# 512-column matmuls for block 1's queries and keys, last merge gates and four output projections, and for the DeltaNet and MoBA output projections

## The reference

```python
# block 1
xn = rmsnorm(h, norm_mix_g)
u = xn @ w_in
q, k, v, xr, gr, ga, gb = split(u)              # 1024 columns each
ya = chunked_band_attention(q, k, v, rel_table) @ w_attn_out
xc = causal_depthwise_conv(xr, conv_w, conv_b)  # 4 taps
hr = rg_lru(xc, w_rg_r, b_rg_r, w_rg_i, b_rg_i, rg_lambda)
yb = (hr * gelu(gr)) @ w_rnn_out
h = h + (sigmoid(ga + b_a) * ya + sigmoid(gb + b_b) * yb) @ w_o
h = h + (silu(g) * up) @ w_ffn_out              # g, up = split(rmsnorm(h) @ w_ffn_in)
# block 2, layer 0: gated DeltaNet; layer 1: MoBA attention
h = h + deltanet(rmsnorm(h)) @ dn_w_out
h = h + relu(rmsnorm(h) @ w_up[0])**2 @ w_down[0]
h = h + moba(rmsnorm(h)) @ mb_w_out
h = h + relu(rmsnorm(h) @ w_up[1])**2 @ w_down[1]
return rmsnorm(h)
```

## Time and profile before

| | |
|---|---|
| median of 3 runs (lowest to highest) | 1134.36 us (1133.88 to 1135.08) |
| the profiled execution | 1135.08 us, with a span of 1133.4 us |
| PE, DVE, ACT, POOL busy in the span | 99%, 67%, 52%, 19% |
| granted clock of PE | 0.999 |
| HBM | 164 GB/s mean |

### The profile page before, as it was taken

One profiled execution on the slowest core, in us unless ns is written; L12 is line 12 of the kernel. 1 busy time (PEld: TensorE's weight loads), 2 busy tenths in 40 slices (PEclk: granted clock), 3 DMA queues, 4 the chain that ended last, 5 costly groups with the idle time before them and its releaser, 6 DMA issues.

```text
span 1133.4 us, 21210 instructions
## 1 busy us (share of the span) xinstructions
PE 1121.4 (99%) x8546; PEld 1072.3 (95%) x8546; DVE 759.0 (67%) x931; ACT 590.0 (52%) x791; POOL 218.1 (19%) x216
## 2 busy tenths in 40 slices
PE   9999999999999999999999999999999999999997
PEld 9999989999888899999999988899999999889997
DVE  6656985676877744699885777754467657776442
ACT  6547557535555543665664556643355446665332
POOL 2995003302000000177843010000030002000000
PEclk9999999999999999999999999999999999999999
DMA  9774442655555555445410355555545445655541
GB/s 286 217 230 149 152 146 96 227 162 186 187 187 195 189 202 170 133 149 186 153 36 1 119 180 185 188 201 177 179 146 186 149 149 153 211 193 186 185 148 38
DMA packets 154995, 187.32 MB, mean 165 GB/s; under 512 B 6544, under 2 KB 143920, under 8 KB 154928
## 3 DMA queue, kind: packets, MB, share of 16 engines
q1 hardware_dynamic: 151360, 184.06, 49.8%
q10 hardware_dynamic: 3568, 2.31, 0.7%
HBM read 185.29 MB, written 1.07 MB: 164 GB/s over the span
## 4 chain that ended last, share of the span: by engine, by line
PE 87%; POOL 5%; DVE 5%; issue 1%; ACT 1%; DMA 0%; DVEq 0%; POOLq 0%; ACTq 0%
PE PS L445 18%; PE PS L386 16%; PE PS L387 16%; PE PS L388 16%; PE PS L447 9%; POOL XN L891 2%; DVE WL L382 2%; POOL TAP L889 2%; POOL XN L886 1%; PE PS L452 1%; PE PS L453 1%; PE PS L454 1%; PE PS L1988 1%; PE PS L2001 1%; PE PS L755 1%
## 5 line engine op out<-in xcount | busy, mean ns | idle before, releaser
L382 DVE TENSOR_TENSOR WL<-RAW,WH 128x2048 fp32r<-128x2048 f32 x170 | 399.9, 2354 | 225.3 <-ACT WH L373 225.2
L373 ACT ACTIVATE WH<-RAW 128x2048 fp32r<-128x2048 f32 x170 | 324.9, 1911 | 227.3 <-PE PS L388 208.1
L445 PE MATMUL PS<-XHL,WH 128*128 128x512 f32 x864 | 300.9, 395 | 0.0
L386 PE MATMUL PS<-XHL,WH 128*128 128x256 f32 x832 | 240.6, 289 | 2.6 <-DVE WL L333 1.4
L447 PE MATMUL PS<-XHL,WL 128*128 128x256 f32 x864 | 239.8, 278 | 0.0
L387 PE MATMUL PS<-XHL,WH 128*128 128x256 f32 x832 | 236.2, 284 | 0.0
L388 PE MATMUL PS<-XHL,WL 128*128 128x256 f32 x832 | 236.2, 284 | 0.0
L445 PEld LDWEIGHTS PS<-XHL,WH 128*128 128x128 f32 x864 | 162.1, 188 | 37.6
L388 PE MATMUL PS<-HH,WL 128*128 (+1 forms) x688 | 194.9, 283 | 0.0
L386 PE MATMUL PS<-HH,WH 128*128 (+1 forms) x688 | 194.9, 283 | 0.0
L387 PE MATMUL PS<-HL,WH 128*128 (+1 forms) x688 | 194.9, 283 | 0.0
(11 more groups left out here) (305 smaller groups left out, 1634.9 us busy)
## 6 DMA issues: line engine op xcount, KB each, us to landing
RAW<-in_mlp_w_up SPq DMA_DIRECT2D x32, 1024.0 KB, 5.4
RAW<-in_mlp_w_down SPq DMA_DIRECT2D x32, 1024.0 KB, 5.0
RAW<-in_w_in SPq DMA_DIRECT2D x25, 1024.0 KB, 5.1
RAW<-in_w_ffn_in_pairs SPq DMA_DIRECT2D x22, 1024.0 KB, 5.1
RAW<-in_dn_w_in SPq DMA_DIRECT2D x16, 1024.0 KB, 5.7
RAW<-in_mb_w_in SPq DMA_DIRECT2D x12, 1024.0 KB, 5.1
RAW<-in_w_ffn_out SPq DMA_DIRECT2D x11, 1024.0 KB, 5.0
RAW<-in_w_attn_out SPq DMA_DIRECT2D x4, 1024.0 KB, 5.8
```

The lines of the kernel that those rows point to most:

```text
L373: act.activation(WH[:, k], RAW[:, k], ACT.Copy).then_inc(hi_done, 1)
L382: dve.tensor_tensor(WL[:, k], RAW[:, k], WH[:, k].bitcast(F32), ALU.subtract).then_inc(lo_done, 1)
L386: pe.matmul(out, wh, xh, start=start, stop=False, skip_group_check=True)
L445: pe.matmul(out.rearrange("p (e t) -> p e t", e=2), h[:, k, part], XHL[:, :, k], start=(k == 0), stop=False, skip_group_check=True)
```

## The change

`multiply_wide` gets the two halves of its moving operand as an argument (`both`), the hook `beside` of `multiply`, and a form with the old products (`halves_` false), used for ro 3. It is called for qk 0 to 7, gab 4 to 7, ao, ro, wo, do and mo, with banks in pairs by the table PAIRS. OH and OL, and DOH and DOL, become halves of one tensor each. The recurrent gates' results go to banks 0 and 1, no longer 3 and 4. ACT copies the right half (`low_to`) to LT, a new buffer of three places in the room of VT (qk), to GAB (gab), or to MU (ao, ro 0 to 2); DVE adds the left half there (`add_to`), and the old read-out works on this sum, out of SBUF. ro 3 is read from its banks as before. In `residual`, DVE adds the right half to H, waits, and adds the left half. The last merge gate is taken after the last gab chunk's copy.

```diff
-    OH = sb("OH", [P, KB, TOK], F32R, Z + 64.25)
-    OL = sb("OL", [P, KB, TOK], F32R, Z + 72.25)
+    LT = sb("LT", [P, SLOTS, 2, TOK], F32, Z + 16)
+    OHL = sb("OHL", [P, 2, KB, TOK], F32R, Z + 64.25)
+    OH, OL = OHL[:, 0], OHL[:, 1]
...
+    DOHL = sb("DOHL", [P, 2, KB, TOK], F32R, Z + 24.5)
...
+        PAIRS = {"qk": (4, 6, 2, 4, 6, 2, 4, 6), "gab": (None, None, None, None, 3, 5, 0, 3), "ao": (5, 0, 2, 4),
+                 "ro": (6, 0, 4, 2), "wo": (6, 4, 2, 6), "do": (6, 4, 2, 6), "mo": (5, 2, 0, 6)}
...
-        def multiply_wide(pe, st, pieces=None, between=None):
+        def multiply_wide(pe, st, pieces=None, between=None, both=XHL, beside=None, halves_=True):
...
+                if not halves_:
+                    mm = product(pe, out[:, 0:TOK], h[:, k, part], l[:, k, part], both[:, 0, k], both[:, 1, k], k == 0, k == KB - 1)
+                    continue
-                pe.matmul(out.rearrange("p (e t) -> p e t", e=2), h[:, k, part], XHL[:, :, k], start=(k == 0), stop=False,
+                pe.matmul(out.rearrange("p (e t) -> p e t", e=2), h[:, k, part], both[:, :, k], start=(k == 0), stop=False,
                           skip_group_check=True)
-                mm = pe.matmul(out[:, TOK:512], l[:, k, part], XH[:, k], start=False, stop=(k == KB - 1),
+                mm = pe.matmul(out[:, TOK:512], l[:, k, part], both[:, 0, k], start=False, stop=(k == KB - 1),
                                skip_group_check=True)
...
+        def low_to(act, st, out):
+            act.wait_ge(mm_done, st.count())
+            act.activation(out, wide_sides(st)[1], ACT.Copy).then_inc(s_.part_out, 1)
+        def add_to(dve, st, out, n):
+            dve.wait_ge(s_.part_out, n)
+            return dve.tensor_tensor(out, out, wide_sides(st)[0], ALU.add)
...
                 if st.j == 0:
                     act.wait_ge(s_.sp_ready, 1)
+                low_to(act, st, LT[:, st.j % SLOTS])
                 gate_pair(st.j)
...
                 merge_gate(2 * st.j - 8)
-                merge_gate(2 * st.j - 7)
+                if st.j < 7:
+                    merge_gate(2 * st.j - 7)
+                act.wait_ge(s_.scanned, 8)
+                low_to(act, st, GAB[:, 2 * st.j:2 * st.j + 2])
+            merge_gate(7)
...
-                dve.wait_ge(mm_done, st.count())
+                lt = LT[:, st.j % SLOTS]
+                ch(add_to(dve, st, lt, part_no("qk") + st.j + 1))
+                ch.wait(dve)
...
-                dve.tensor_tensor(out, tiles(bank(st)), rows_, ALU.mult).then_inc(freed[st.slot], 1)
+                dve.tensor_tensor(out, tiles(lt), rows_, ALU.mult).then_inc(freed[st.slot], 1)
...
-                read_out(st, GAB[:, 2 * st.j:2 * st.j + 2])
+                blk = slice(2 * st.j, 2 * st.j + 2)
+                ch(add_to(dve, st, GAB[:, blk], part_no("gab") + st.j - 3))
+                ch.wait(dve)
+                dve.tensor_tensor(GAB[:, blk], GAB[:, blk], by_rows(2), ALU.mult).then_inc(freed[st.slot], 1)
...
-                    dve.tensor_tensor(hb, hb, bank(st), ALU.add).then_inc(freed[st.slot], 1)
+                    ch(dve.tensor_tensor(hb, hb, wide_sides(st)[1], ALU.add))
+                    ch.wait(dve)
+                    dve.tensor_tensor(hb, hb, wide_sides(st)[0], ALU.add).then_inc(freed[st.slot], 1)
...
-                multiply(pe, st, XH, XL)
+                multiply_wide(pe, st)
+                if j == 0:
+                    pe.wait_ge(freed[0], 2)
                 pe.wait_ge(s_.conv_done, j + 1)
...
-            steps(pe, seg["v"], lambda st: multiply(pe, st, XH, XL, tokens_out=True))
+            for st in (Step(seg["v"], j, None) for j in range(4)):
+                if st.j < 2:
+                    pe.wait_ge(s_.gates_done, 14 + 2 * st.j)
+                multiply(pe, st, XH, XL, tokens_out=True)
...
+            steps(pe, seg["ao"], lambda st: multiply_wide(pe, st, both=OHL))
+            steps(pe, seg["ro"], lambda st: multiply_wide(pe, st, (s_.y_done, 0) if st.j == 0 else None, halves_=st.j < 3))
+            steps(pe, seg["wo"], lambda st: multiply_wide(pe, st, (s_.ml_done, 0) if st.j == 0 else None, both=OHL))
```

More of the change, by code:

```diff
@@ L438, in multiply_wide @@
             for n, (b, k) in enumerate(order_of(pieces)):
+                if n == 4 and beside:
+                    beside()
                 if n == KB and between:
@@ L1039, in low_half, with part_no @@
             act.activation(two(SG[:, st.slot]), wide_sides(st)[1], ACT.Copy).then_inc(s_.low_out, 1)
+        def part_no(name):
+            return {'qk': 0, 'gab': 8, 'ao': 12, 'ro': 16}[name]
+        def low_to(act, st, out):
[4 more added lines that the diff above has]
+            return dve.tensor_tensor(out, out, wide_sides(st)[0], ALU.add)
         def add_halves(dve, st, earlier):
@@ L1158, in _ @@
                     mix_high(st.j - 1)
+                if st.j < 3:
+                    act.wait_ge(freed[(seg["ao"].first + st.j) % SLOTS], (seg["ao"].first + st.j) // SLOTS + 1)
+                    low_to(act, st, MU[:, 2 * st.j:2 * st.j + 2])
             mix_high(3)
@@ L1506, in _ @@
                 dve.tensor_tensor(XL[:, blk], XN[:, blk], XH[:, blk].bitcast(F32), ALU.subtract).then_inc(s_.y_done, 1)
-                dve.wait_ge(mm_done, st.count())
+                ch(add_to(dve, st, MU[:, blk], part_no("ao") + j + 1))
                 dve.wait_ge(s_.gab_done, 8)
-                dve.tensor_tensor(MIX[:, 2 * j:2 * j + 2], bank(st), GAB[:, 2 * j:2 * j + 2], ALU.mult).then_inc(freed[st.slot], 1)
+                ch.wait(dve)
+                dve.tensor_tensor(MIX[:, blk], MU[:, blk], GAB[:, blk], ALU.mult).then_inc(freed[st.slot], 1)
             def mix_lo(p):
@@ L1520, in _ @@
                     mix_lo(st.j - 1)
-                dve.wait_ge(mm_done, st.count())
-                dve.tensor_tensor(MU[:, blk], bank(st), GAB[:, 8 + 2 * st.j:10 + 2 * st.j], ALU.mult).then_inc(freed[st.slot], 1)
+                if st.j < 3:
+                    ch(add_to(dve, st, MU[:, blk], part_no("ro") + st.j + 1))
+                    ch.wait(dve)
+                    sum_ = MU[:, blk]
+                else:
+                    dve.wait_ge(mm_done, st.count())
+                    sum_ = wide_sides(st)[0]
+                dve.tensor_tensor(MU[:, blk], sum_, GAB[:, 8 + 2 * st.j:10 + 2 * st.j], ALU.mult).then_inc(freed[st.slot], 1)
                 dve.wait_ge(freed[st.slot], st.base // SLOTS + 1)
@@ L1880, in _ @@
                 for r in range(2):
-                    mm = pe.matmul(PS[:, 3 + j % 2, r * TOK:(r + 1) * TOK], WRI[:, r, j], XN[:, j], start=True, stop=True)
+                    mm = pe.matmul(PS[:, j % 2, r * TOK:(r + 1) * TOK], WRI[:, r, j], XN[:, j], start=True, stop=True)
                 mm.then_inc(s_.rg_done, 1)
-            steps(pe, seg["v"], lambda st: multiply(pe, st, XH, XL, tokens_out=True))
+            for st in (Step(seg["v"], j, None) for j in range(4)):
+                if st.j < 2:
+                    pe.wait_ge(s_.gates_done, 14 + 2 * st.j)
+                multiply(pe, st, XH, XL, tokens_out=True)
             c = seg["v"].first - 1
@@ L2098, in _ @@
             head_sums(3)
-            steps(pe, seg["do"], lambda st: multiply(pe, st, DOH, DOL, None if st.j else (s_.yy, 0),
-                                                     beside=None if st.j else last_rows))
+            steps(pe, seg["do"], lambda st: multiply_wide(pe, st, None if st.j else (s_.yy, 0), both=DOHL,
+                                                          beside=None if st.j else last_rows))
             def mlp(layer):
@@ L2127, in _ @@
             attn_pv(pe, 11)
-            steps(pe, seg["mo"], lambda st: multiply(pe, st, OH, OL, None if st.j else (s_.ol_done, 8)))
+            steps(pe, seg["mo"], lambda st: multiply_wide(pe, st, None if st.j else (s_.ol_done, 8), both=OHL))
             mlp(1)
```

18 lines of the change are left out of this document (8 added, 10 removed).

## The result

The changed kernel took 1137.77 us in the median of 7 runs (1136.85 to 1140.09), against 1134.36 before (7 runs, 1133.39 to 1135.08); the ratio is 1.0031, with a 95% interval of 1.0022 to 1.0041. I had forecast 1134.2 with a range up to 1136.6: it is slower, outside the range. The same kernel taken again, in another set of 11 runs, gave 1135.88 (1134.42 to 1138.75), a ratio of 1.0014 (1.0005 to 1.0023). So its times spread over 5.7 us in 18 runs, where the 27 runs of the kernel before beside the second set stay within 1.4 (1133.81 to 1135.2). That spread is part of the result. In two later sets the kernel before had a far run too, 1136.57 among 19 and 1137.59 among 14; neither was profiled.

The account below looks back on a forecast made before the run. PE, busy 99% of the span with 87% of the chain, was taken as the bound. Saved 3.8 less lost 3.65 (qk 2.4, seams 1.25) gave 0.15 faster: 1134.2 us on the median's level, range 1131.8 to 1136.6.

Parts of the forecast that it names:

- PE's saving: Converted chunks shorten PE's stream by 0.21 us each fast, 0.10 slow; with gab's 0.3, 3.8 us saved.
- fast, fast, slow: Pitch in ao, ro, wo: ao 4 and ro 3 chunks save 1.47 us, wo behind narrow ro 3 saves 0.41.
- qk: PE waits for POOL; seven DVE multiplications of two SBUF operands stop POOL 0.35 us each, 2.4 lost; PE's gain worthless.
- gab: gab 4 to 7: added ACT and DVE work delays gab 7's start to 195.7; 0.3 us of gain left.
- Seams: Into the MLPs after wo, do, mo: second residual add, 0.72 later against 0.30 slack, loses 0.42 each, 1.25 together.
- The step that failed: PE's wide pairs: 0.3536 us behind a narrow stream, until a float32 matmul comes between; then 0.3469.
- the slow pitch as a rival: Converted pairs run slow everywhere, being short runs between narrow ones: 1.9 us less saved, 1136.1; chance 0.12.
- the net: Whole kernel: 3.8 us saved less 3.65 lost, 0.15 faster.

Follow-up runs that it names:

- second profile: The unaltered changed kernel profiled again, from its set of 11 runs: 1135.59 us, a span of 1133.9.
- first profile: The changed kernel, profiled in the slowest of its first seven runs: 1140.09 us, a span of 1138.2.
- the control: Kernel before plus one unused DVE multiplication per qk chunk, reading the PSUM bank and the row factors: 1134.19 us, ratio 1.0.

## Why the prediction was wrong

- **PE's saving.** Right where the stream was fast: -0.83 in mo against -0.84, and -0.64 in do against -0.63, in the second profile. In ao, ro and wo one profile had slow ao and ro and fast wo, the other slow throughout, against my fast, fast, slow: -1.59 and -1.18 against -1.88. ao and ro were slow because gab 5 and 6 before them were, straight behind float32 attention matmuls and with no wait that the trace shows, in all six profiles with these chunks wide, and because the wait in gab 7 left it so; and wo, behind the narrow ro 3, was fast in the second. In the other four of the six, gab 7 to ro 3 gave -1.51, against the 1.47 that I had for ao and ro.
- **qk.** Right in mechanism and size: +2.43 and +2.60 against 2.4. Six of the seven multiplications cost POOL 0.31 or 0.32 (as 1.05 less 0.74; the seventh falls together with L383), against my 0.35, and one PSUM operand in its place gives it back. The other 0.09 of the longer blocks (7.17 less 6.77) is L383, which costs POOL 2.01 at L901 and cost 1.92 at L886. v 0 starts at 88.17 (88.1 forecast). That the shorter PE chunks are worth nothing here was nearly right: 0.29 with the sum in PSUM.
- **gab.** PE's start of gab 7 at 195.67 against 195.7 forecast. The gain of the stage is 0.16, not 0.3, as gab 5, 6 and 7 ran slow.
- **Seams.** I had 0.42 each, by a slack of 0.30 that the second add uses up; the stages are +0.41 to +0.47 in the second profile, and PE waits at L611 as forecast. In the first they are +2.59, +1.90 and +0.41, together 4.90 where I had 1.25.
- **The step that failed** is the one before all these: "That slower pitch lasted in this trace until a float32 matmul came between". I took the state behind a float32 matmul to be always fast, and the 54 wide chunks of fi, u0 and u1 that the change does not touch to be safe. At the norm sums without a wait that held, fast behind them 17 times of 17. It did not hold behind the attention matmuls in front of gab 5, nor behind the gate matmuls of qk (qk 1 to 7 all slow in the first profile), where it cost little. And the change puts a wait there, which I had forecast myself and priced at 0.42 only, with nothing for the pitch behind it. With the wait the pitch two chunks on was that in front of it 12 times of 12, and in front it differs from execution to execution. A slow segment costs 2.1 (fi) or 1.5 (u0, u1), together 3.6 of the 4.3 us by which the first profile's span is over the second's (1138.2 against 1133.9). The rest is mostly slow chunks in wo and do. I had priced the slow pitch as a rival, but for 18 converted chunks only (1136.1), and in a chance of 0.12.
- Without that the net is what the terms said, a little on the other side: the second profile's span is 0.5 us over before's, where I had 0.15 under.

What I cannot say: how often the changed kernel draws which pitch, and so what made up the 3.4 us by which the first set's median is over the kernel before. Only profiles show it, and I have two of it. Nor do the runs show why the same wait ends at one pitch or the other.

## What to carry to other kernels

A DVE operation that is moved from PSUM to SBUF operands can cost another engine more than it costs DVE: where POOL works on the critical chain, keep one of two operands in PSUM, for instance by writing a sum back into its bank. Before a long stream of matmuls is called untouched by a change, its pitch must be compared too, pair by pair, since a wait or a single small matmul in front of it or inside it can set it for the whole rest. And where a kernel's runs spread wider after a change than before, take a second profile before explaining the first.

## What the runs showed of the hardware

A stream of pairs of a 512-column and a 256-column fp32r matmul ran at two stable pitches at the same granted clock of 1.0, that is at 2.4 GHz: starts 112, 233, 117, 231 ns apart over two pairs and then again, 346.5 ns a pair; or 114, 232, 118, 241, 120, 235 over three pairs, 353.3 ns a pair. I had expected one. A stream kept its pitch as long as nothing interrupted it, and could change it where float32 matmuls did or where PE waited, as in gab 7 and do 0. In the kernel before, one matmul of 128 columns more in front of each of three streams cost 6 us, two cost 1.6, and behind a stall one more gave 4.8 us back. It held for all the 20 chunks that followed in fi. Why the two exist stays open: nothing tried here reaches below the spacing of the starts. What the table above says in short, for the norm sums and two chunks on: without a wait, no or two matmuls more turn slow into fast and one more keeps slow; with a wait, the pitch stays with no matmul more and turns over with one more. That is the order of the cases seen, not an explanation of them.

A float32 matmul of 128 columns shows in the trace as two records of 0.11 us; the expectations took it for one. The four records of the norm sums are two matmuls, and so are the four of L1881 in each qk chunk, which the description of the kernel calls four.

A DVE operation with both inputs in SBUF held POOL up, by 0.31 us of its 0.72 (L1503) and by 2.01 of 2.29 (L383); with one input in PSUM it held up nothing, as the run with the sum in PSUM and the control show.
